# The even layer's normed heads: attention weights transposed by a DMA in place of TensorE

## The reference

```
u    = rms_norm(h, ln_even)
proj = u @ w_in_even                      # qa ka va qb kb vb gate
qa   = rope(rms_norm(qa, a_q_norm))       # 8 heads x 128
ka   = rope(rms_norm(ka, a_k_norm))       # 2 key heads
p    = softmax(qa @ ka.T / sqrt(128))     # 256 x 256 per head, no mask
ya   = p @ va                             # 4 query heads share a key/value head
yb   = diff_attention(qb, kb, vb)         # the next 8 heads: difference of two softmaxes
h    = h + (concat(ya, yb) * silu(gate)) @ w_out_even
```

## Time and profile before

| | |
|---|---|
| median of 3 runs | 3051.84 us |
| the profiled execution, whole | 3051.91 us |
| its span in the profile | 3049.7 us |
| TensorE busy, all of the span | 3037.2 us |
| VectorE busy (61%) | 1873.4 us |
| ScalarE busy (49%) | 1487.0 us |
| the four head groups' stretch, 2188.4 to 2299.4 us: VectorE, ScalarE busy | 88.3 and 66.9 of 111.0 us |

### The profile page before, as it was taken

How to read it: one execution, slowest core, us unless ns; L and a number is a source line. 1 busy time by engine, 2 the same in 40 slices (tenths; PEclk the granted TensorE clock), 3 DMA queues, 4 the chain that set the end, 5 groups by cost and what they waited for, 6 DMA issues and landing times.

```text
span 3049.7 us, 48366 instructions
## 1 busy us (share of the span) xinstructions
PE 3037.2 (100%) x20858; PEld 2822.0 (93%) x20858; DVE 1873.4 (61%) x2279; ACT 1487.0 (49%) x1763; POOL 135.9 (4%) x132
## 2 busy tenths in 40 slices
PE   9999999999999999999999999999999999999999
PEld 9889999999999999989888888889998889999987
DVE  7875554445445567776555555556787666767663
ACT  6664433333333457755443443445565654555553
POOL 0001000000000011110000000002000001101000
PEclk9999999999999999999999999999999999999999
DMA  6444545555545554454555555555434455555554
GB/s 236 127 147 166 175 171 180 180 172 175 179 169 182 175 187 176 159 207 177 196 185 188 192 180 195 180 193 188 172 139 158 175 180 180 179 193 188 175 192 151
DMA packets 107316, 542.71 MB, mean 178 GB/s; under 512 B 38368, under 2 KB 38880, under 8 KB 44384
## 3 DMA queue, kind: packets, MB, share of 16 engines
q1 hardware_dynamic: 77264, 532.14, 49.8%
q10 hardware_dynamic: 29840, 7.49, 1.4%
HBM read 530.15 MB, written 2.10 MB: 175 GB/s over the span
## 4 chain that ended last, share of the span: by engine, by line
PE 97%; DVE 1%; ACT 1%; DMA 1%; issue 0%; SPq 0%; ACTq 0%; DVEq 0%
PE PB L1171 29%; PE PB L1172 15%; PE PB L1196 14%; PE PB L1195 14%; PE PB L1197 14%; PE PB L1190 2%; PE PB L1191 2%; PE PB L1192 2%; PE PB L1182 1%; PE PB L1180 1%; PE PB L1181 1%; PE PB L1253 1%; DMA raw<-in_mla_in 1%; PE PB L1318 1%; DVE WLt L1831 0%; PE PB L1319 0%
## 5 line engine op out<-in xcount | busy, mean ns | idle before, releaser
L1831 DVE TENSOR_TENSOR WLt<-raw,WHt 128x2048 fp32r<-128x2048 f32 (+2 forms) x506 | 1139.3, 2259 | 760.4 <-ACT WHt L1425 760.0
L1425 ACT ACTIVATE WHt<-raw 128x2048 fp32r<-128x2048 f32 (+2 forms) x506 | 954.9, 1889 | 1102.7 <-PE PB L1172 583.7
L1171 PE MATMUL PB<-Xt,WHt 128*128 128x512 f32 x2880 | 1027.6, 395 | 0.0
L1172 PE MATMUL PB<-Xt,WLt 128*128 128x256 f32 x2880 | 808.5, 281 | 0.0
L1171 PEld LDWEIGHTS PB<-Xt,WHt 128*128 128x128 f32 x2880 | 540.8, 188 | 109.8
L1195 PE MATMUL PB<-Xt,WHt 128*128 128x272 f32 (+1 forms) x2192 | 634.6, 290 | 2.6 <-DVE WLt L1831 1.3
L1196 PE MATMUL PB<-Xt,WHt 128*128 128x272 f32 (+1 forms) x2192 | 630.0, 287 | 0.0
L1197 PE MATMUL PB<-Xt,WLt 128*128 128x272 f32 (+1 forms) x2192 | 626.8, 286 | 0.0
L1172 PEld LDWEIGHTS PB<-Xt,WLt 128*128 128x128 f32 x2880 | 543.5, 189 | 0.1
L1195 PEld LDWEIGHTS PB<-Xt,WHt 128*128 128x128 f32 x2192 | 412.6, 188 | 11.9 <-DVE WLt L1831 4.5
L1196 PEld LDWEIGHTS PB<-Xt,WHt 128*128 128x128 f32 x2192 | 413.2, 189 | 1.1 <-issue 0.2
(11 more groups left out here) (267 smaller groups left out, 2870.9 us busy)
## 6 DMA issues: line engine op xcount, KB each, us to landing
raw<-in_gu SPq DMA_DIRECT2D x176, 1024.0 KB, 4.8
raw<-in_dn SPq DMA_DIRECT2D x88, 1024.0 KB, 4.8
raw<-in_odd_in SPq DMA_DIRECT2D x64, 1024.0 KB, 4.8
raw<-in_even_in SPq DMA_DIRECT2D x52, 1024.0 KB, 4.8
raw<-in_lru_in SPq DMA_DIRECT2D x24, 1024.0 KB, 4.8
raw<-in_mla_o SPq DMA_DIRECT2D x16, 1024.0 KB, 4.8
raw<-in_lru_o SPq DMA_DIRECT2D x16, 1024.0 KB, 4.8
raw<-in_even_o SPq DMA_DIRECT2D x16, 1024.0 KB, 5.0
```

Source lines behind the costliest of these rows:

```text
L1171: t.matmul(o, wh, both, start=first, stop=False)
L1172: m = t.matmul(o[:, 0, :], wl, ah, start=False, stop=last)
L1425: a.activation(hi, r, ACT.Copy).then_inc(s_hi, 1)
L1831: v.tensor_tensor(lo, r, hi.bitcast(f32), sub).then_inc(s_lo, 1)
```

## The change

The eight normed heads no longer use TensorE, a bank or the identity for the transposition. `even_planes` (ScalarE) copies the 512 floats per partition of `E1` as 1024 halfwords into two planes in `sqt`; `even_cross` issues the transposing DMA on ScalarE's queue into `acct`; `even_weave` (ScalarE, two copies of 512 halfwords) puts the two planes together in `vA`, then copies the high part to `TTH`, and VectorE subtracts from `vA` for `TTL`. `E1` is free when the planes are copied. The order in the list becomes:

- end of N: `q_step`, then, for q > 0, the weave of the former group's head a and the planes of its head b
- end of N+1: the DMA of the former group's b, then the scores of head a
- end of N+2: the values of the former group's head a, the weave of its b, then the planes of the new head a
- inside N+3: the DMA of head a, the scores of head b; end of N+3: the values of the former group's head b

For the last group (q = 3, N = 373) the same steps fall at the ends of 377 (weave of 6, planes of 7, ahead of the scores of head 8), 378 (DMA of 7), 379 (values of 6, weave of 7, ahead of the transposition of head 8 and the scores of head 9) and 380 (values of 7).

```diff
+    def even_weave(hd):
+        p.mark("even woven", "even woven", hd)
+        p.mark("trh", "trh", hd)
+        p.mark("trl", "trl", hd)
+        p.step("even_weave", hd, now["TT2"])
...
-        p.step("weigh_split", hd, vj, ("out", "tr", hd) if stage_[0] == "e" else ("trl", hd), vready)
+        p.step("weigh_split", hd, vj, ("trl", hd), vready)
...
             rope2(("qA", q), "q", q_in)
+            if q:
+                even_weave(("e", 2 * q - 2))
+                even_planes(("e", 2 * q - 1))
...
-        p.inside(3, 1, lambda s=s, q=q: (t_step(("e", 2 * q)), s(1)))
-        p.after(4, lambda v=v, q=q: (v(0), t_step(("e", 2 * q + 1))))
-        p.after(5, lambda v=v: v(1))
+        p.after(2, lambda a=a: even_planes(a))
+        p.inside(3, 1, lambda s=s, a=a: (p.step("even_cross", a), s(1)))
+        if q == 3:
+            p.after(4, lambda a=a, b=b: (even_weave(a), even_planes(b)))
+        p.after(5, lambda b=b: p.step("even_cross", b))
+        p.after(6, lambda v=v, b=b: (v(0), even_weave(b)))
+        p.after(7, lambda v=v: v(1))
...
+            def even_planes(hd):
+                a.wait_ge(*when("pp", hd))
+                if hd[1]:
+                    a.wait_ge(s_even_crossed, 16 * hd[1])
+                a.activation(EVEN_PLANES.bitcast(u16).rearrange("p (a n) -> p a n", a=2), halfwords(E1),
+                             ACT.Copy).then_inc(sems["even planes"], 1)
+
+            def even_cross(hd):
+                a.wait_ge(*when("even planes", hd))
+                if hd[1]:
+                    a.wait_ge(*when("even woven", ("e", hd[1] - 1)))
+                x = EVEN_CROSSED.bitcast(u16).rearrange("p (g n) -> p g n", n=128)
+                a.dma_start(x, EVEN_PLANES.bitcast(u16), transpose=True).then_inc(s_even_crossed, 16)
+
+            def even_weave(hd, free):
+                a.wait_ge(s_even_crossed, 16 * (hd[1] + 1))
+                if hd[1]:
+                    a.wait_ge(*when("trl", ("e", hd[1] - 1)))
+                for i in range(2):
+                    x = EVEN_CROSSED.bitcast(u16)[:, 512 * i:512 * i + 512].rearrange("p (q k n) -> p k q n", q=2, k=2)
+                    w = EVEN_WOVEN.bitcast(u16).rearrange("p (k q n a) -> p a k q n", k=2, q=2, a=2)[:, i]
+                    m = a.activation(w, x, ACT.Copy)
+                m.then_inc(sems["even woven"], 1)
+                a.wait_ge(*when(*free))
+                a.wait_ge(*when("even woven", hd))
+                a.activation(TTH, EVEN_WOVEN, ACT.Copy).then_inc(sems["trh"], 1)
...
+            def even_weave(hd, free):
+                v.wait_ge(*when("trh", hd))
+                v.tensor_tensor(TTL, EVEN_WOVEN, TTH.bitcast(f32), sub).then_inc(sems["trl"], 1)
```

More of the change, by code:

```diff
@@ L671, in t_step @@
         now["E1"] = ("tr", hd)
+    def even_planes(hd):
+        p.mark("even planes", "even planes", hd)
+        p.step("even_planes", hd)
+        now["E1"] = ("even planes", hd)
+    def even_weave(hd):
[3 more added lines that the diff above has]
+        p.step("even_weave", hd, now["TT2"])
     def weave(hd):
@@ L750, in make_plan @@
         p.after(0, q_step)
+        a, b = ("e", 2 * q), ("e", 2 * q + 1)
         if q == 0:
@@ L1006, in build_program @@
         MLA_PLANES, MLA_CROSSED = (sqt[:, 0:384], acct[:, 0:384]), tab[:, 960:1344]
+        EVEN_PLANES, EVEN_CROSSED, EVEN_WOVEN = sqt[:, 0:512], acct[:, 0:512], buf["vA"]
         PLANES, CROSSED, WOVEN = buf["kA"], (buf["vA"], buf["Vp"]), buf["TT2"]
@@ L1040, in build_program @@
         s_mla_crossed = ctx.enter_context(nc.semaphore("s_mla_crossed"))
+        s_even_crossed = ctx.enter_context(nc.semaphore("s_even_crossed"))
         s_crossed = ctx.enter_context(nc.semaphore("s_crossed"))
@@ L1764, in _ @@
                     crossed(*x)
+                elif what == "even_planes":
+                    even_planes(*x)
+                elif what == "even_cross":
+                    even_cross(*x)
+                elif what == "even_weave":
+                    even_weave(*x)
                 elif what == "uq_out":
```

## The result

The changed kernel takes 3070.41 us (median of 3 runs, 3069.29 to 3071.23) against 3051.84 (3051.52 to 3052.61): 18.6 us slower, a ratio of 1.006 with a 95% interval of 1.0047 to 1.0073. The profiled execution has a span of 3068.3 us.

The account below looks back on a forecast made before the run. TensorE was taken to bound the kernel, so each new wait costs in full: 19.0 us of new waits less 4.7 that go, 14.3 us slower than before, 3066 us, range 3055 to 3074.

Parts of the forecast that it names:

- The likeliest case: Whole kernel: new waits of TensorE outweigh what goes, 14.3 us slower, 3066 us; chance 0.50.
- The wait at tile 3: Units 369, 373, 377: TensorE waits for the bank of b's values, 2.6 us each, 7.8 us together.
- The score pair: Scores of head a: TensorE waits for the rotated queries, 1.2 us once and 0.66 twice, 2.5 us together.
- The edge: Unit 381, at the difference heads: TensorE waits for head 7's bank, 8.4 us, 2.9 of it at tile 2.
- Small waits ahead of unit 381: Edge to the difference heads, before the large stall: small waits of TensorE, 0.3 us.
- Costed at nothing: Changed stretch: the DMA's issue, 1.25 us of ScalarE's queue, and its landing, 2.7 to 5.5 us, add no time.
- The half clock: TensorE behind its stalls: no slowdown to 1.2 GHz counted in the sum, only allowed for as a rival in unit 381.
- rival C: Unit 381 runs on at 1.2 GHz behind its stall: up to 5.65 us, middle 2.8, 3069 us; chance 0.15.
- the 1.2 that it let go: Old waits that go: 0.6 us ahead of head 0's transposition, some 0.6 for rotated queries before later score pairs.
- A: Changed stretch: the waits don't come, VectorE reaches `gated` in time; 4.1 to 4.7 us off, 3047.5 us; chance 0.15.
- B: Bank waits don't bite; next period's score pair (2.6 us) and head 9's transposition (5.2) wait; +7, 3059 us; chance 0.12.
- D: ScalarE becomes the bound: copies or DMA waits 1 us more a head, some 20 us, 3072; chance 0.08.

Follow-up runs that it names:

- low_late_3: `copied_after_3` with VectorE's low split of unit N+5 put behind the values of the former head b; 3066.7 us.
- weave_early_3: `copied_after_3` with b's DMA issued directly behind b's planes and its weave one unit later behind a's scores, apart from `TTH` and `TTL`; 3064.7 us.
- bank_first_3: `copied_after_3` with the list of free banks turned by three, so the bank of b's values goes to the next group's tile 0; 3078.0 us.
- last_two_by_pe_3: `copied_after_3` with heads 6 and 7 transposed by TensorE as before the change, heads 0 to 5 through the DMA; 3058.9 us.
- copied_after_3: The changed kernel with all 40 transposing DMAs replaced by copying DMAs of the same bytes, the transposition left out; 3071.5 us.
- after: The changed kernel itself, against the kernel before the change; 3070.4 us, ratio 1.0047 to 1.0073.
- roots_first_3: `copied_after_3` with ScalarE's high split put behind the query roots at the end of each period's first unit; 3069.2 us.
- filled_3: `copied_after_3` with overwritten fp32 matmuls ahead of the late banks, 8 in units 369, 373 and 377, 28 in unit 381; 3072.9 us.

## Why the prediction was right, and where its number was luck

The likeliest case was right in sign, place and size: 3066 for 3070.4, inside the range. Step by step:

- *The wait at tile 3.* 2.6 us each forecast, 2.26, 2.30 and 2.36 measured. The order on VectorE was as walked, and `low_late_3`, `weave_early_3` and `bank_first_3` show the mechanism from three sides. The walk is closer than these numbers say. With T at 2228.03, TensorE could have gone on at 2237.04 (2236.92 and 0.12), T+9.0 as forecast, and started at 2239.45, T+11.4 for the forecast 11.6: between starts the wait is 2.4. Of the 0.2, 0.1 is the two weaving copies (1.4, not 1.5).
- *The score pair.* 1.2 and 2 x 0.66 forecast; 1.11, 0.57 and 0.62 measured.
- *The edge.* 2.9 + 5.5 forecast, 2.68 + 4.75 measured; `last_two_by_pe_3` shows that it goes with the two heads.
- *Small waits ahead of unit 381.* 0.3 forecast; the rows show none.
- *Costed at nothing.* The DMA, its issue and its landing: right (`copied_after_3`). The planes took 1.04 us, 1.05 assumed. The trace of the changed kernel has 3.1 us from issue to landing, in the median, for a head's eight blocks. The Trainium skill ("VectorE: DVE Perf Modes", The three transpose paths) states 1309 ns for one block, and eight times that, an estimate, is 10.5 us; the measurement decides. How the prediction came from there to 21 us it doesn't show, and nothing rests on it.
- *The half clock.* This is the term that was mis-sized: 4.1 us measured. The forecast put it at nothing and left it to rival C (unit 381 alone, 2.8 us in the middle, 3069). It came, with 2.4 us in unit 381, and 1.7 more in unit 377, behind a wait of only 2.36 us, where no step had it. The Trainium skill ("TensorE: Matmul & The Clock Gate", Why this matters for your kernels) names gaps in mid-kernel as what sends the engine back to half rate; these rows agree in kind.

So the forecast and rival C were both true. The forecast counted waits between starts: 19.0 new ones less the 1.2 that it let go, 17.8. Counted so, the eight new waits come to 18.0 and those that went to 1.3, a growth of 16.7 (15.9 as the rows draw idle time). The forecast had 1.1 too much, and that covered part of the 4.1 us of half clock and 0.3 of restarts, which were missing. Without that luck the sum would have been 5.4 too low; it was 4.3, 1.0 of which lies ahead of the stretch.

Of the rivals, A (the waits don't come) is out by the stalls. B (only the score waits bite) is out by the stalls at the fourth tile, and by `bank_first_3`: the bank decides. D (ScalarE's copies longer) is out by the rows: none took longer than assumed, and 0.8 us less of issue a head changed nothing.

## What to carry to other kernels

When work is moved from a full engine to two half-empty ones, walk their queues in order rather than their busy shares: an operation that waits holds up everything queued behind it, here the one that gives a bank free. Each idle gap of a TensorE that was never idle may also cost it the full clock: price it. A step that is right in the steady part can be wrong at the stage's edge; here two heads of eight cost nearly half, and treating the last ones differently is a small change.

## What the hardware showed that I had not expected

- The clock doesn't answer equal waits equally. Of 11 waits of 2.17 to 2.42 us at the fourth tile, in `after` (3), `copied_after_3` (3), `roots_first_3` (3) and `last_two_by_pe_3` (2), the granted clock fell to 0.50 behind 6: one, three, two and none. In `low_late_3` it fell behind a wait of 2.06 us and not behind one of 1.98. Behind those of 3.4 us and more (`bank_first_3`) it fell each time, behind the 0.8 of `weave_early_3` never. What decides between equal ones these runs don't show.
- A copying DMA of the same 256 KB between the same tiles took ScalarE's queue 0.47 us to issue, the transposing one 1.25; landing 2.3 and 3.1.
- An fp32 matmul with 256 columns took 0.41 us (`filled_3`) against 0.12 between the starts of an fp32r one.
